# Row halves for the attention scores of a hybrid decoder step: 64 rows of one kv group as both operands, instead of 128 rows with a masked query

## The chip, the cores and the metric

One core of a Trainium2 chip runs the whole program. The metric is the device time of one execution in microseconds (us): the median of 3 runs for the kernel before. The core has five engines that run side by side and meet at semaphores: PE (TensorE, matrix multiply; its weight loads are listed apart, as PEld), DVE (VectorE), ACT (ScalarE), POOL (GpSimd) and SP (SyncE, which here only issues DMAs). Durations of single instructions are given in nanoseconds (ns).

## The reference, cut to what matters

The model computes one step of a decoder trunk for a prompt of 1024 tokens and for 8 samples of 8 tokens. There are 8 query heads in 2 kv groups (4 heads each) of head dimension 64. The change touches the prompt's local attention: for every query token and head, a softmax over the keys of the selected blocks ("sel") and one over a sliding window of 512 ("win"):

```python
def local_attend(q, pos, idx, valid, kv_g, kw, kw_pos):
    ...
    s = jnp.einsum('tghd,tgkd->tghk', q, ks) * SCALE          # sel scores
    o_sel = jnp.einsum('tghk,tgkd->tghd', masked_softmax(s, m_sel).astype(vs.dtype), vs)
    ...
    s = jnp.einsum('tghd,kgd->tghk', q, kw[:, 0]) * SCALE      # win scores
    o_win = jnp.einsum('tghk,kgd->tghd', masked_softmax(s, m_win).astype(kw.dtype), kw[:, 1])
```

A score sums over the 64 dimensions `d` of one kv group `g` only. At 1024 tokens there are 16 blocks of 64 and 16 are selected, so for the prompt the selected branch is plain causal attention over all earlier tokens.

## The kernel before, in words

The program runs in stages: projections, a set-up stage (compressed attention, sums and masks), the prompt's local attention, the samples' attention, then output projection and FFN. Each engine has its own instruction list written out by hand, with semaphores between them. There is no scheduler: the order in the lists is the order of the work.

**Layout.** Queries lie transposed in `qT[:, tile, j, :]`: 128 partitions, of which rows 0 to 63 hold head `j` of kv group 0 and rows 64 to 127 head `j` of group 1, by 128 tokens. Keys lie transposed the same way in `ksT` (selected branch) and `kwT` (window branch): rows 0 to 63 are group 0, rows 64 to 127 group 1.

**Loops.** The prompt attention goes over 8 query tiles of 128 tokens (`QTile`, from i = 7, the tile with the most keys, down to i = 0), and in each over j = 0 to 3. Each (tile, j) has passes. For i of 4 or more there are four: sel group 0, sel group 1, win group 0, win group 1, one unit each. For i below 4 there are two, sel and win, and each holds two units, group 0 and group 1, whose scores go to two neighbouring PSUM banks. That makes 64 passes for i = 7 to 4, and 8 passes for each of i = 3, 2, 1 and 0: 96 in all.

**One step of PE** (`step_of` in `prompt_pe`): turns (`turn`, L778) and applications (`apply`, L790) of the present pass in groups of up to 4 blocks; then the first turn of the next pass; then `scores` (L764) of the pass that is three ahead; then the last `apply` of the present pass. So a group of score matmuls has transposes before it and `apply` matmuls behind it. `scores` issues one matmul for each unit and each 512 columns of keys: 8 blocks of 128 keys make two of 512, a window of 5 blocks makes 512 and 128. All of this is float32, and the profile shows two MATMULs and two LDWEIGHTS for each float32 matmul (a transpose has one).

**The query.** Before the change the sum over 64 dimensions is made with all 128 rows: POOL's `take_q` (L848) makes two copies of the query tile, `q_cur[0]` and `q_cur[1]`, each multiplied by a column `own_rows[:, g]` that is 1 in the rows of its own group and 0 in the others, and `scores` multiplies `q_cur[g]` with all 128 rows of the keys. `own_rows` is filled by four memsets of DVE at the end of the set-up stage (L603). POOL makes the tile of the next j when `s_done` says that the last scores of this j are done, and PE waits for `q_ready` before the first scores of a j.

**Behind the scores.** DVE adds the causal mask and takes the maximum (`highest`, L911 to L916), ACT takes the exponential (`soften`, L873), PE turns the probabilities, DVE and ACT copy them out of PSUM in turns (`save_group`, L829 on DVE and L862 on ACT), PE applies the values, DVE mixes (L928 to L938).

Of the kernel before, what the change touches and what calls it, by code (L numbers as in the profile page):

```python
# [21 lines left out]
ALU = mybir.AluOpType  # L22
# [3 lines left out]
P = 128  # L26
# [12 lines left out]
H, G, HPG, HD = 8, 2, 4, 64  # L39
# [111 lines left out]
def program(nc, a, out):  # L151
    ctx = ExitStack()
    with ctx:
        sem_names = {}

        def sem(name):
            if name not in sem_names:
                sem_names[name] = ctx.enter_context(nc.semaphore(name))
            return sem_names[name]
# [116 lines left out]
        rp = Region(work_at)  # L276
        probs = [rp(SEQ) for _ in range(2)]
        p_cmp_p = arena[:, work_at:work_at + NT * H * NC_P].rearrange("p (t g n) -> p t g n", t=NT, g=G)
        pT = [rp(4, P) for _ in range(2)]
        q_cur = [rp(P) for _ in range(G)]  # L280
        own_rows = rp(G)
        neg_m = rp(4)
        row_sum = rp(4)
        coef = rp(4)
# [27 lines left out]
        def const(name):  # L312
            o, w = CONST[name]
            return cst[:, o:o + w] if o < NEARLY else late[:, o - NEARLY:o - NEARLY + w]
# [31 lines left out]
        def bank(b):  # L346
            return psum[:, b, :]
# [141 lines left out]
        def setup_dve(dve, step, rotate):  # L489
# [4 lines left out]
            for c in range(2):  # L494
                ins = nc.vector.tensor_tensor(
                    prod_p[:, :, c * KV:(c + 1) * KV].rearrange("p t (g d) -> p t g d", g=G),
                    z_all[:, 0:NT, c * KV:(c + 1) * KV].rearrange("p t (g d) -> p t g d", g=G),
                    pos_rep[:, c, :].unsqueeze(1).unsqueeze(1).broadcast_to([P, NT, G, HD]), ALU.mult)
# [7 lines left out]
            for g in range(G):  # L506
                r = slice(g * HD, (g + 1) * HD)
                for b in range(SB):
                    ins = nc.vector.tensor_copy(q_bd[r, b, g * 32:(g + 1) * 32].rearrange("p (j t) -> p j t", j=HPG),
                                                qT[r, NT, :, b * ST:(b + 1) * ST])  # L510
# [17 lines left out]
            for g in range(G):  # L528
                r = slice(g * HD, (g + 1) * HD)
                ins = nc.vector.tensor_copy(ckT_p[r, g, :], bank(6)[r, 0:NC_P])  # L530
# [22 lines left out]
            for i in range(NT):  # L553
                for g in range(G):
                    ins = nc.vector.tensor_tensor(pc[:, i, g * HPG:(g + 1) * HPG],
                                                  bank(4 + i // 2)[:, i % 2 * 256:(i % 2 + 1) * 256].rearrange("p (h g n) -> p g h n", g=G, n=NC_P)[:, g],
                                                  const("cmp_mask")[:, i * NC_P:(i + 1) * NC_P].unsqueeze(1).broadcast_to([P, HPG, NC_P]), ALU.add)
# [6 lines left out]
            for g in range(G):  # L564
                for j in range(HPG):
                    ins = nc.vector.tensor_copy(cv_bd[j * NC_P:(j + 1) * NC_P, g, j * HD:(j + 1) * HD], cv_p[0:NC_P, g * HD:(g + 1) * HD])
# [9 lines left out]
            for b in range(SB):  # L576
                ins = nc.vector.max(m8[0:NS, b, :], cand[0][0:NS, b, :])
            step(ins)
            for b in range(SB):
                ins = nc.vector.match_replace(cand[1][0:NS, b, :], m8[0:NS, b, :], cand[0][0:NS, b, :], -1.0)  # L580
            step(ins)
            step(nc.vector.memset(cand[1][0:NS, :, NCAND:NCAND + 3], 1e30))
            for b in range(SB):
                ins = nc.vector.max(m8[0:NS, SB + b, :], cand[1][0:NS, b, :])
            step(ins)
            for b in range(SB):
                ins = nc.vector.match_replace(cand[2][0:NS, b, :], m8[0:NS, SB + b, :], cand[1][0:NS, b, :], -1.0)
# [10 lines left out]
            step(nc.vector.reciprocal(cmp_sum, cmp_sum))  # L598
            step(nc.vector.tensor_tensor(cmp_sum.rearrange("p (t h) -> p t h", t=NT), cmp_sum.rearrange("p (t h) -> p t h", t=NT),
                                         z_all[:, 0:NT, ZKV - NGATE:ZKV].rearrange("p t (h r) -> p t h r", r=3)[:, :, :, 0], ALU.mult))  # L600
            for g in range(G):
                for h in range(G):
                    nc.vector.memset(own_rows[h * HD:(h + 1) * HD, g:g + 1], 1.0 if g == h else 0.0)  # L603
            nc.vector.memset(coef, 0.0).then_inc(setup_dve_done, 1)

            for i in range(NT):
                dve.wait_ge(pc_applied, i + 1)
                for g in range(G):
                    c = i * H + g * HPG
                    ins = nc.vector.tensor_tensor(mixT[:, 0:HPG, i * P + g * HD:i * P + (g + 1) * HD],  # L610
                                                  bank(i)[:, g * 256:(g + 1) * 256].rearrange("p (j d) -> p j d", j=HPG),
                                                  cmp_sum[:, c:c + HPG].unsqueeze(2).broadcast_to([P, HPG, HD]), ALU.mult)
# [45 lines left out]
        def pooling_act(act):  # L658
# [6 lines left out]
        s_done, m_ready, p_ready, t_done, pv_done, o_used, q_ready = (sem(n) for n in (  # L665
            "s_done", "m_ready", "p_ready", "t_done", "pv_done", "o_used", "q_ready"))
# [82 lines left out]
        def prompt_pe(pe):  # L749
            pe.wait_ge(setup_dve_done, 11)  # L750

            def scores(qt, j, p):
                x = p % 2
                if p == 0:

                    pe.wait_ge(q_ready, j + (4 * qt.pos + 1))

                pe.wait_ge(p_ready, qt.count(j, p) + 1)
                for u, (kind, g) in enumerate(qt.passes[p]):
                    kT = ksT if kind == "sel" else kwT  # L760
                    k0, n = qt.keys[kind]
                    for c in range(0, n * P, 512):
                        w = min(512, n * P - c)
                        ins = pe.matmul(bank(2 * x + u + c // 512)[:, 0:w], q_cur[g],  # L764
                                        kT[:, k0 * P + c:k0 * P + c + w], start=True, stop=True)
                ins.then_inc(s_done, 1)

            def turn(qt, j, p, n):

                x = p % 2  # L770
                y, half, _ = qt.group(j, p, n)
                if n == 0:

                    pe.wait_ge(p_ready, qt.count(j, p) + 3)

                pe.wait_ge(pT_saved[y], half + 1)
                for m, block in enumerate(qt.groups[p][n]):
                    ins = pe.transpose(bank(4 + y)[:, m * P:(m + 1) * P], probs[x][:, block[4]:block[4] + P], ident)  # L778
                ins.then_inc(t_done, 1)

            def apply(qt, j, p, n):
                x = p % 2
                y, half, _ = qt.group(j, p, n)
                pe.wait_ge(pT_saved[y], half + 2)
                if n == 0:

                    pe.wait_ge(o_used, qt.count(j, p) + 1)
                for m, (u, kind, g, kt, _) in enumerate(qt.groups[p][n]):
                    c0 = (KVR if kind == "sel" else 2 * KVR) + KV + g * HD
                    ins = pe.matmul(bank(6 + x)[:, u * HD:(u + 1) * HD], pT[y][:, m, :], z_all[:, kt, c0:c0 + HD],  # L790
                                    start=(kt == qt.keys[kind][0]), stop=(kt == qt.i))
                if n == len(qt.groups[p]) - 1:
                    ins.then_inc(pv_done, 1)

            def step_of(qt, j, p):

                for n in range(1, len(qt.groups[p])):
                    turn(qt, j, p, n)
                    apply(qt, j, p, n - 1)
                nxt, ahead = later(qt, j, p, 1), later(qt, j, p, 3)  # L800
                if nxt:
                    turn(*nxt, 0)
                if ahead:
                    scores(*ahead)
                apply(qt, j, p, len(qt.groups[p]) - 1)

            scores(q_tiles[0], 0, 0)
            scores(q_tiles[0], 0, 1)
            turn(q_tiles[0], 0, 0, 0)
            scores(q_tiles[0], 0, 2)  # L810
            every_pass(pe, step_of)

            pe.wait_ge(o_used, NPASS + 2)
            pe.wait_ge(pT_saved[0], n_groups // 2 + 1)
            pe.wait_ge(pT_saved[1], n_groups // 2 + 1)
            for i in range(NT):
                y = i % 2
                if i >= 2:
                    pe.wait_ge(heads_saved[y], i // 2)
                for k in range(HPG):  # L820
                    ins = pe.transpose(bank(4 + y)[:, k * P:(k + 1) * P], mixT[:, k, i * P:(i + 1) * P], ident)
                ins.then_inc(heads_turned[y], 1)
# [17 lines left out]
        def prompt_pool(pool, behind_first):  # L840

            pool.wait_ge(setup_dve_done, 11)
            qT_flat = qT.rearrange("p t j n -> p (t j) n")

            def take_q(n):

                for g in range(G):
                    ins = nc.gpsimd.tensor_tensor(q_cur[g], qT_flat[:, n, :] if isinstance(n, int) else  # L848
                                                  qT_flat[:, bass.ds(n, 1), :].rearrange("p a n -> p (a n)"),
                                                  own_rows[:, g:g + 1].broadcast_to([P, P]), ALU.mult)  # L850
                ins.then_inc(q_ready, 1)

            take_q(0)
            behind_first()
            for qt in q_tiles:
                with pool.Fori(0, HPG) as j:

                    pool.wait_ge(s_done, qt.count(j, qt.np - 1) + 1)
                    take_q(j + (HPG * qt.pos + 1))
# [1298 lines left out]
```

## Time and profile before

| What | Value |
|---|---|
| median of 3 runs | 1720.71 us (1719.9 to 1721.72) |
| the profiled execution, its own time | 1720.44 us |
| its span, first to last instruction | 1718.6 us |
| mean granted TensorE clock | 0.948 |
| PE busy | 1557.8 us, 91% of the span |
| prompt attention on the time line | about 351 to 641 us |

The span is what the trace covers; the execution's own time is 1.8 us longer. Each row of the profile is for one engine: start, duration, line of the kernel, operation, output and inputs with shapes. "128\*64 128x512" on a matmul means 128 active rows and 64 active columns of the array (the weights), and a moving operand of 128 rows by 512 columns. A matmul's listed duration contains its run through the array and overlaps the next; what it costs in a stream is the distance from its start to the next start. The row of the clock (PEclk) is in tenths of full speed.

### The profile page before, as it was taken

The numbers are of one execution on the slowest core, as the hardware profiler recorded it, in microseconds if no ns is written. First come the engines' busy times: TensorE is split into PE (matmuls) and PEld (weight loads), VectorE is DVE, ScalarE is ACT, GpSimd is POOL, SyncE is SP. The second block draws the span as 40 slices with busy tenths as digits, with TensorE's granted clock in tenths as the row PEclk, the third lists the DMA queues.
The fourth block names the chain that finished last, engine by engine and source line by source line (L and its number), as shares of the span: only waits on it lengthen the run. The fifth ranks groups of instructions, "written<-read, shape, count | busy, mean of one in ns | idle before, by whom it ended". The sixth has DMA issues, their size and how long they took to land.

```text
span 1718.6 us, 26090 instructions
## 1 busy us (share of the span) xinstructions
PE 1557.8 (91%) x9892; PEld 1018.6 (59%) x9892; DVE 781.8 (45%) x1532; ACT 519.9 (30%) x936; POOL 258.3 (15%) x287
## 2 busy tenths in 40 slices
PE   6588985599999988999898999999999999999993
PEld 3244443478887885666354666666666665666662
DVE  5799965567777783665655111111111120100105
ACT  5133220034444544554333122222222221111105
POOL 2244317100000010010320111111111110000002
PEclk9799996599999999999898999999999999999996
DMA  8666632020000005566211111111111111121102
GB/s 365 211 217 210 198 95 84 0 98 1 1 1 1 1 1 220 221 252 190 86 49 35 46 49 49 49 49 49 49 49 49 49 53 48 48 54 34 34 0 116
DMA packets 93460, 146.37 MB, mean 85 GB/s; under 512 B 3691, under 2 KB 74831, under 8 KB 91143
## 3 DMA queue, kind: packets, MB, share of 16 engines
q1 hardware_dynamic: 81823, 78.43, 14.6%
q0 software_dynamic: 11520, 67.11, 11.1%
q8 instruction: 38, 0.62, 0.1%
q14 instruction: 23, 0.19, 0.0%
q10 hardware_dynamic: 56, 0.01, 0.0%
HBM read 135.91 MB, written 14.04 MB: 87 GB/s over the span
## 4 chain that ended last, share of the span: by engine, by line
PE 77%; DVE 15%; DMA 3%; issue 2%; ACT 1%; POOL 1%; SPq 0%; DVEq 0%; POOLq 0%; ACTq 0%
PE psum L1501 43%; PE psum L764 6%; PE psum L790 6%; PE psum L1468 6%; DVE arena L2000 4%; DVE arena L1999 4%; PE psum L778 3%; PE psum L1106 2%; PE psum L1047 2%; PE psum L1059 2%; DMA arena<-in_cache_kv_cmp,cmp_idx 2%; PE psum L1085 1%; PE psum L2070 1%; DMA arena<-in_w_in 1%; PE psum L448 1%
## 5 line engine op out<-in xcount | busy, mean ns | idle before, releaser
L1501 PE MATMUL psum<-arena 128*128 128x384 f16 (+1 forms) x4752 | 734.7, 318 | 5.4 <-POOL arena L1446 2.8
L1501 PEld LDWEIGHTS psum<-arena 128*128 128x128 f16 x4752 | 466.3, 98 | 273.6 <-issue 10.4
L1738 DVE SCALAR_TENSOR_TENSOR arena<-psum,arena 128x384 f32<-128x384 f32 (+1 forms) x66 | 35.3, 535 | 349.2 <-ACT arena L1607 349.2
L2070 PE MATMUL psum<-arena 128*128 128x512 f16 (+1 forms) x768 | 153.6, 361 | 0.0
L790 PEld LDWEIGHTS psum<-arena 128*128 128x128 f32 x1056 | 137.1, 194 | 11.8 <-issue 6.7
L790 PE MATMUL psum<-arena 128*128 128x64 f32 x1056 | 138.7, 268 | 0.0
L1607 ACT ACTIVATE arena<-psum 128x384 f32<-128x384 f32 (+1 forms) x66 | 31.3, 474 | 338.1 <-PE psum L1501 338.1
L764 PE MATMUL psum<-arena 128*128 128x512 f32 (+3 forms) x384 | 130.1, 462 | 1.7 <-DVE arena L610 1.7
L1446 POOL TENSOR_TENSOR arena<-arena 128x384 f32 (+1 forms) x66 | 57.7, 874 | 465.3 <-ACT arena L1609 465.3
L2070 PEld LDWEIGHTS psum<-arena 128*128 128x128 f16 x768 | 76.3, 99 | 73.1 <-issue 5.3
L873 ACT ACTIVATE arena<-psum,arena 128x640 f32<-128x640 f32 (+7 forms) x128 | 89.2, 700 | 56.8 <-DVE arena L916 55.3
L1707 DVE SCALAR_TENSOR_TENSOR arena<-arena 128x2816 f16<-128x2816 f32 x8 | 24.7, 3092 | 173.7 <-ACT arena L1583 173.7
L1468 PE MATMUL psum<-arena 128*128 128x512 f16 (+1 forms) x432 | 97.4, 387 | 4.9 <-POOL arena L1436 4.9
L1850 POOL DMA_INDIRECT arena<-in_cache_kv_cmp,cmp_idx x64 | 78.5, 1226 | 147.7 <-DVE arena L2000 105.2
L778 PE MATMUL psum<-arena 128*128 128x128 f32 x528 | 88.8, 277 | 5.7 <-ACT arena L873 5.7
L764 PEld LDWEIGHTS psum<-arena 128*128 128x128 f32 x384 | 64.5, 191 | 39.8 <-issue 35.1
L916 DVE TENSOR_REDUCE arena<-psum 128x1 f32<-128x640 f32 (+7 forms) x96 | 85.5, 891 | 3.3
L862 ACT ACTIVATE arena<-psum 128x256 f32<-128x256 f32 (+2 forms) x92 | 43.2, 469 | 124.2 <-PE psum L778 117.6
L1632 ACT ACTIVATE arena<-psum 128x384 f32 (+3 forms) x24 | 11.4, 473 | 217.1 <-PE psum L1501 217.1
L1468 PEld LDWEIGHTS psum<-arena 128*128 128x128 f16 (+1 forms) x432 | 43.4, 101 | 55.9 <-POOL arena L1436 5.1
L1172 ACT ACTIVATE arena<-psum 128x512 f32<-128x512 f32 (+2 forms) x104 | 53.1, 557 | 73.8 <-PE psum L1047 47.5
L1703 DVE SCALAR_TENSOR_TENSOR arena<-arena 128x2048 f16<-128x2048 f32 x22 | 50.4, 2292 | 52.3 <-ACT arena L1579 52.3
(259 smaller groups left out, 1643.8 us busy)
## 6 DMA issues: line engine op xcount, KB each, us to landing
arena<-in_w_gate SPq DMA_DIRECT2D x22, 512.0 KB, 4.0
arena<-in_w_up SPq DMA_DIRECT2D x22, 512.0 KB, 5.2
arena<-in_w_down SPq DMA_DIRECT2D x8, 1408.0 KB, 7.1
arena<-in_x_prompt SPq DMA_DIRECT2D x16, 512.0 KB, 3.6
arena<-in_w_in SPq DMA_DIRECT2D x8, 908.0 KB, 12.1
arena<-in_cache_kv_win SPq DMA_DIRECT2D x8, 512.0 KB, 3.3
out_y_prompt<-arena SPq DMA_DIRECT2D x8, 512.0 KB, 2.6
out_kv_win_sample<-in_cache_kv_win SPq DMA_DIRECT2D x1, 4032.0 KB
```

What stands on the lines that cost most here:

```text
L764: ins = pe.matmul(bank(2 * x + u + c // 512)[:, 0:w], q_cur[g], kT[:, k0 * P + c:k0 * P + c + w], start=True, stop=True)
L778: ins = pe.transpose(bank(4 + y)[:, m * P:(m + 1) * P], probs[x][:, block[4]:block[4] + P], ident)
L790: ins = pe.matmul(bank(6 + x)[:, u * HD:(u + 1) * HD], pT[y][:, m, :], z_all[:, kt, c0:c0 + HD], start=(kt == qt.keys[kind][0]), stop=(kt ...
L873: ins = nc.scalar.activation(probs[x][:, u * 512:u * 512 + n], S, ACT.Exp, bias=neg_m[:, 2 * x + u:2 * x + u + 1], accum_out=row_sum[:, 2 ...
L916: nc.vector.tensor_reduce(neg_m[:, 2 * x:2 * x + nu], S[:, :, 0:n * P], AX, ALU.max, negate=True).then_inc(m_ready, 1)
L1446: nc.gpsimd.tensor_tensor(row(1), silu_out[c][:, 0:c1 - c0], row(0), ALU.subtract).then_inc(act_ready, 1)
L1468: ins = pe.matmul(bank(2 * s + h)[0:n, :], mix_slot[s][xp][:, k, 0:n], w_out[wp][:, k, 512 * h:512 * (h + 1)], start=(k == 0 and i == 0), ...
L1501: ins = pe.matmul(out[:, 0:c1 - c0], w[wp][:, k, :], x[xp][:, k, c0:c1], start=(k == 0 and i == 0), stop=(k == n_k - 1 and i == 2))
L1850: nc.gpsimd.indirect_dma_start(raw[k % RAW].rearrange("p c r -> p (c r)"), None, cmp_rows, bass.IndirectOffsetOnAxis(ap=cmp_idx[:, k:k + 1 ...
L1999: step(nc.vector.tensor_tensor(rows, rows, pos, ALU.mult))
L2000: nc.vector.tensor_tensor(cmp_acc, cmp_acc, raw[k % RAW], ALU.add).then_inc(prod_free, 1)
L2070: ins = pe.matmul(dst[:, 0:n], hT[s][xp][:, k, :], w_in[wp][:, k, c0:c0 + n], start=(k == 0 and i == 0), stop=(k == KD - 1 and i == 2))
```

## The change

The 64-row slice `r` of group g is taken from both operands: the query tile and the keys. The zeros are no longer needed, so POOL makes one plain copy of the query tile in place of two masked ones, and the four memsets of `own_rows` go. What is computed is the same. A matmul whose operands start at partition 0 or 64 and have 64 rows addresses the upper or the lower half of the array's rows.

```diff
-        q_cur = [rp(P) for _ in range(G)]
-        own_rows = rp(G)
+        q_cur = rp(P)
...
-            for g in range(G):
-                for h in range(G):
-                    nc.vector.memset(own_rows[h * HD:(h + 1) * HD, g:g + 1], 1.0 if g == h else 0.0)
             nc.vector.memset(coef, 0.0).then_inc(setup_dve_done, 1)
...
                 for u, (kind, g) in enumerate(qt.passes[p]):
                     kT = ksT if kind == "sel" else kwT
                     k0, n = qt.keys[kind]
+                    r = slice(g * HD, (g + 1) * HD)
                     for c in range(0, n * P, 512):
                         w = min(512, n * P - c)
-                        ins = pe.matmul(bank(2 * x + u + c // 512)[:, 0:w], q_cur[g],
-                                        kT[:, k0 * P + c:k0 * P + c + w], start=True, stop=True)
+                        ins = pe.matmul(bank(2 * x + u + c // 512)[:, 0:w], q_cur[r],
+                                        kT[r, k0 * P + c:k0 * P + c + w], start=True, stop=True)
...
             def take_q(n):
 
-                for g in range(G):
-                    ins = nc.gpsimd.tensor_tensor(q_cur[g], qT_flat[:, n, :] if isinstance(n, int) else
-                                                  qT_flat[:, bass.ds(n, 1), :].rearrange("p a n -> p (a n)"),
-                                                  own_rows[:, g:g + 1].broadcast_to([P, P]), ALU.mult)
-                ins.then_inc(q_ready, 1)
+                nc.gpsimd.tensor_copy(q_cur, qT_flat[:, n, :] if isinstance(n, int) else
+                                      qT_flat[:, bass.ds(n, 1), :].rearrange("p a n -> p (a n)")).then_inc(q_ready, 1)
```

## Rows read from the trace of the kernel before

**Rows 1.** The page: PE's busy time and the granted clock in 40 slices.
```profile
PE 1557.8 (91%) x9892; PEld 1018.6 (59%) x9892; DVE 781.8 (45%) x1532; ACT 519.9 (30%) x936; POOL 258.3 (15%) x287
PEclk9799996599999999999898999999999999999996
```

**Rows 2.** Stretch, its us, busy of PE, PEld, DVE, ACT, POOL; PEclk, DMA, GB/s.
```profile
353.00:542.00 189.00, 187.77 (x1305) 152.14 (x1304) 143.75 (x398) 86.51 (x185) 11.45 (x31) 1.00 0.05 22
542.00:602.00 60.00, 60.00 (x399) 47.63 (x397) 44.25 (x114) 29.65 (x80) 6.08 (x16) 1.00 0.00 1
602.00:622.00 20.00, 19.80 (x151) 18.66 (x150) 17.27 (x51) 9.91 (x34) 3.23 (x9) 1.00 0.00 0
622.00:641.00 19.00, 14.82 (x107) 13.13 (x105) 16.44 (x62) 9.91 (x45) 3.61 (x10) 0.91 0.01 2
676.00:816.00 140.00, 136.33 (x1181) 88.88 (x1179) 82.24 (x219) 73.83 (x147) 10.54 (x24) 0.98 0.62 224
```

**Rows 3.** Waits from 542 to 641 us: waiter, releaser, us, times, longest.
```profile
PE psum L778 <- ACT arena L873: 4.0, 9, 0.8
```

**Rows 4.** Time line of PE, i = 7 and then i = 3: start, us, instruction.
```profile
367.89 0.55 PE L790 MATMUL psum<-arena 128*128 128x64 f32 x4
368.28 0.39 PE L778 MATMUL psum<-arena 128*128 128x128 f32 x2
...
559.14 0.61 PE L778 MATMUL psum<-arena 128*128 128x128 f32 x4
559.59 1.88 PE L764 MATMUL psum<-arena 128*128 128x512 f32 x4
561.31 1.00 PE L790 MATMUL psum<-arena 128*128 128x64 f32 x8
562.14 0.61 PE L778 MATMUL psum<-arena 128*128 128x128 f32 x4
```

**Rows 5.** Time line at 298 us: 64-row matmuls, and weight loads in a stream.
```profile
298.07 3.67 PE L440 MATMUL psum<-arena 64*64 64x512 f32 x4 [8.87 <-DVE arena L547]
```

**Rows 6.** Time line of PE in the samples' stage, 690.70 to 690.95 us.
```profile
690.53 0.27 PE L1088 MATMUL psum<-arena 128*128 128x128 f32 x1
690.73 0.27 PE L1089 MATMUL psum<-arena 64*128 64x64 f32 x1
```

**Rows 7.** Time line of PE, samples' stage: 64-row matmuls between 128-row ones.
```profile
693.15 0.43 PE L1117 MATMUL psum<-arena 64*64 64x129 f32 x2
693.51 0.43 PE L1118 MATMUL psum<-arena 128*64 128x128 f32 x2
693.87 1.09 PE L1047 MATMUL psum<-arena 128*128 128x128 f32 x8
```

**Rows 8.** Time line of PE, samples' stage: column halves, and what follows them.
```profile
696.29 1.08 PE L1059 MATMUL psum<-arena 128*64 128x512 f32 x4
697.30 0.66 PE L1085 MATMUL psum<-arena 128*128 128x128 f32 x4
697.79 1.04 PE L1047 MATMUL psum<-arena 128*128 128x128 f32 x8
```

**Rows 9.** Time line of PE, samples' stage: from column halves to a 64-column matmul.
```profile
700.35 1.10 PE L1106 MATMUL psum<-arena 128*64 128x129 f32 x16
701.38 0.43 PE L1073 MATMUL psum<-arena 128*128 128x64 f32 x2
701.66 1.04 PE L1047 MATMUL psum<-arena 128*128 128x128 f32 x8
```

**Rows 10.** Time line at the end of the set-up stage.
```profile
339.17 0.35 DVE L603 MEMSET arena<- 64x1 f32 x4
...
339.68 9.29 PE L463 MATMUL psum<-arena 128*128 128x256 f32 x32 [10.25 <-DVE arena L604]
```

**Rows 11.** POOL's copies of the query tile, and the next scores (i = 0).
```profile
634.12 0.76 POOL L848 TENSOR_TENSOR arena<-arena 128x128 f32<-128x128 f32 x2 [3.00 <-PE psum L764]
...
635.37 0.62 PE L764 MATMUL psum<-arena 128*128 128x128 f32 x4
```

## The prediction

> **What bounds the kernel now.** I read the page first: PE is busy for 91% of the span, and the granted clock is full, outside the set-up stage [rows 1]. Then the table of stretches over the attention stage, because the change lives there: from 353 to 602 us PE is busy for all but 1.2 of 249 us at clock 1.00, DVE for about 75% of it and ACT for less than half [rows 2]. So up to 602 us (tiles i = 7 to 2) whatever PE is given or spared moves the end one for one. From 602 to 622 (i = 1) PE still has 19.8 of 20, but DVE 17.3. From 622 (i = 0) PE is busy 14.8 of 19 and waits 4.0 us, nine times, for ACT's exponential [rows 2, 3]: there a ring of scores, maximum, exponential and turn sets the pace. Last I read the time line of PE, by distances from start to start, in the stage and in the samples' stage, where this kernel already uses 64-row and 64-column matmuls.
>
> **What a score pass costs now.** A 512-column pass of i = 3 is four MATMULs (two matmuls, two passes through the array each) and takes 561.31 - 559.59 = 1.72 us, 0.43 each; the four transposes before it take 0.45 (0.11 each), and the scores begin right behind them [rows 4]. The eight `apply` MATMULs behind take 0.83, and four of them 368.28 - 367.89 = 0.39, so the pace is 0.11 and the first step only 0.05 to 0.06: the first weight loads were made under the scores. A row count of 64 does not shorten a matmul by itself: four of 64x64 by 512 last 3.67 us at the half clock (1.2 GHz) of that stretch, and 4 x 0.43 doubled is 3.42; the 0.25 left is the first load and the run through the array [rows 1, 4, 5]. So what the change can give or take lies in the seams between the forms, and in whether two halves run at once.
>
> **Term 1, the seam into the scores.** Today turn, scores and apply all use the array as 128 by 128. Afterwards scores use 64 rows and their neighbours 128. The trace has this very step: a 128-column transpose with 128 rows, then one with 64 rows, 0.20 us apart, where 0.11 is the distance without a change of form [rows 4, 6]: 0.09 lost. Then the first weight load is no longer under the matmul before: two 64-row MATMULs of 129 columns, with one change of form, take 693.51 - 693.15 = 0.36, and the next pair 0.36 again, where two without a change take 0.22 [rows 7]: 0.14 in all. For the 128-column weights of the scores I take 0.15: 0.093 and a load of 0.056 (L1085: four from 697.30 to 697.79 are 0.49, not 0.436) [rows 8].
>
> **Term 2, the seam out.** Behind the last score comes `apply` with 128 rows. The wait for the array is again 0.095: four 512-column MATMULs of L1059 and the step to L1085 take 1.01, of which two times 0.427 is streaming, 0.055 the exposed load and 0.10 this seam [rows 8]. `apply` moves only 64 columns, so its loads hide worse: after a change of form two such MATMULs take 701.66 - 701.38 = 0.28 [rows 9]; in today's stream the first two take 0.39 - 2 x 0.11 = 0.17 [rows 4]. That is 0.11 more (0.105 unrounded), and the seam out is 0.20.
>
> Together 0.35 us a pass. The three score groups ahead of the loop include two in a row, so there are 95 pairs of seams: 63 in i = 7 to 4, 8 in each of the others. For i = 7 to 4 each pass has one unit; its two matmuls lie in the same half and one behind the other, so nothing is won: 63 x 0.348 = **+21.9 us**. The least that one could argue for is the wait for the array alone, 0.19 a pass; the most, by the 0.36 steps of [rows 7] and one more exposed load for `apply`, 0.40. I take 0.35, whose parts each have a row.
>
> **Term 3, two halves at once.** For i below 4 a pass has both units, group 0 in the upper rows and bank 2x, group 1 in the lower rows and bank 2x+1. No row shows two row halves at once. The nearest show two column halves: four 512-column MATMULs in 1.01 with seam and load, where 1.71 would be the streaming alone, and sixteen of 129 columns in 701.38 - 700.35 = 1.03, 0.064 each instead of 0.11 [rows 8, 9]. Both pairs run at once, though in L1059 both MATMULs of the first half stand ahead of those of the second in the list. The bounds for rows: nothing, or half of the scores' time. I take half, nearest to these rows. i = 3: 8 x (0.348 - 0.854) = **-4.05**. i = 2 (384 columns, 4 x 0.32 = 1.28): 8 x (0.348 - 0.642) = **-2.35**; DVE is at 74 to 75% there [rows 2], so it can follow: a pass of i = 3 falls from 4.28 to about 3.8 with about 3.1 of DVE. i = 1 (256 columns): 8 x (0.348 - 0.43) = -0.65, of which I count **-0.3**, since DVE had only 2.7 of 20 us left. i = 0: PE would pay 0.35 - 0.21, but it waits 4.0 us there anyway; on the ring the scores start 0.15 later and end 0.21 sooner: **0**.
>
> The Trainium skill, TensorEngine Tiling (Array Packing), Key Properties, states that changing the tiling mode, not just the tile, drains the array: the rule that speaks against this change; the steps of 0.20 in [rows 6] agree, and it gives no price. By the same page's theoretical factor of 2 for a dimension of 64 alone one would write off the scores' time to half and forget terms 1 and 2. TensorE: Matmul & The Clock Gate, Part 3, says that a weight load overlaps a running matmul only where the row group differs; by that each one-unit pass would lose three more loads of 0.055, about 10 us in all and 1746. The trace disagrees: in [rows 5] all four have the same rows, and 0.25 beside the streaming has no room for three more loads (0.11 each at that clock).
>
> **Term 4, the rest.** The four memsets of DVE stand ahead of the semaphore for which PE waits 10 us (L463), directly on the path: 0.35 with gaps, 339.17 to 339.56, **-0.4** [rows 10]. POOL's two masked copies (0.76) become one plain copy. No row has a POOL copy of this shape; it lies between nothing and the 0.76 of two, I take about half. It costs nothing either way: POOL starts at 634.12 and the scores that need it at 635.37, in the shortest passes of all, so 1.25 us cover it [rows 11]; if the copy took longer than that, each j of i = 0 would wait for the excess.
>
> **Sum.** +21.9 - 4.05 - 2.35 - 0.3 - 0.4 = +14.8 us. On the profiled execution: 1720.44 (span 1718.6 and 1.84 around it) + 14.8 = 1735.2; that execution is 0.3 under the median, so **1735.5 us** against 1720.71. The likeliest case's own range: a seam pair of 0.32 to 0.40 gives 1733 to 1740.
>
> **Rivals.**
> A. *Row halves don't run at once.* For it: only column halves are seen at once, and row halves share the 128 output columns. Against: they write different banks, and the order in the list did not matter in L1059. Term 3 turns into a loss: 16 x 0.35 for i = 3 and 2 = 5.6, i = 1 up to 2.8, i = 0 about 0.15 a pass on the ring, 1.2: +21.9 + 9.6 - 0.4 = +31, **1752 us** at most, 1749 if i = 1 and 0 hide half. The Trainium skill, TensorE: Matmul & The Clock Gate, Part 3, has four row tiles of 32 at 3.07 times, which speaks against A; no row here shows it.
> B. *The seams are cheap, and it gets faster.* The place is the transpose before and the `apply` behind each score group; the price is 0.35 a pass by the rows, and if halving the rows alone (columns stay 128) let neighbours flow through, it would be near zero. Then -6.8 (i = 3) - 5.1 (i = 2) - 1.5 (i = 1 and 0, DVE and ring) - 0.4 = -14, **1707 us**. It decides at 14 us over some 80 passes that PE bounds: below 0.17 us a pass the kernel is faster. For it: only one of the rows has 128 columns on both sides. Against: exactly that one shows 0.20 [rows 6]. With 0.19 a pass (the wait for the array, loads hidden) it comes out at 1722.
> C. *The array isn't addressed in halves at all*, the instruction just runs with 64 rows live: no seam, no pairs, 0.4 from the memsets, **1720.3 us**. Against it: the 64-row forms of L1117 and L1089 do have seams.
> D. *The clock falls*, half the array being idle in two passes of three. The samples' stage, full of column halves, kept 0.98 [rows 2], and the scores are about a third of the time. If it fell to 1.2 GHz for a fifth of the stage, some 30 us more, 1765.
>
> **How the numbers follow.** Forecast 0.70, A 0.14, B 0.07 (0.03 of it the cheap but not free seam at 1722), C 0.04, D 0.03, rest 0.02 on the slow side. The range should reach A: 1729 to 1752, which leaves out B, C and D, and the ends of the forecast's neighbours. The measurement tells 0.2%, 3.4 us, from no change. Slower: 0.70 + 0.14 + 0.03 + 0.02 = 0.89. Same: C and half of the cheap seam, 0.05. Faster: the rest, 0.06.
>
> **What would show it.** In the changed trace: L764 with 64 active rows; from the last L778 to the first L764 0.20 instead of 0.11, and the second score MATMUL 0.055 later than its streaming time; from the last L764 0.095 beyond its streaming, and the first two L790 0.16 apart. Passes of i = 7 to 4 longer by 0.35 each, in i = 3 four score MATMULs in about 0.91 + 0.1 instead of 1.72. PE's stage starts 0.4 earlier and ends about 14.8 later. It is wrong if the first L764 of a group stands 0.11 behind the transpose (B or C), if in i = 3 the MATMULs are 0.43 apart one by one (A), or if PEclk leaves 1.00 between 353 and 602 (D).

## The result, and the profile after

The changed kernel takes 1929.07 us (median of 4, 1927.8 to 1933.4) against 1720.31: 1.1216 times as long, 95% interval 1.1197 to 1.1236, or 208.8 us more, where 14.8 were forecast. The profiled execution took 1928.32 us with a span of 1926.5. In several kernels below single executions fall into two groups 190 us apart; a ratio with an interval is then over the faster group, and the text gives the single times.

The page of the changed kernel; the rows answer to [rows 1], and the last three are groups of instructions (busy us, mean ns | idle before).

```profile
PE 1768.1 (92%) x9892; PEld 1142.0 (59%) x9892; DVE 784.0 (41%) x1528; ACT 513.1 (27%) x936; POOL 243.0 (13%) x254
PEclk9899975655555555989998989999999999999996
...
L787 PE MATMUL psum<-arena 128*128 128x64 f32 x1056 | 225.1, 375 | 0.0
L761 PE MATMUL psum<-arena 64*128 64x512 f32 (+3 forms) x384 | 203.2, 735 | 1.2 <-DVE arena L606 1.2
...
L775 PE MATMUL psum<-arena 128*128 128x128 f32 x528 | 132.2, 380 | 4.6 <-ACT arena L867 4.5
```

The clock row shows where the time went. In slices 9 to 16 of 40 it reads 5 where it read 9 before; the rest of the row is much as it was. It isn't the scores (L761) alone that grew: `apply` (L787), untouched by the change, has a mean of 375 ns where it had 268, and the turns (L775) 380 for 277. The stretches of the stage, which answer to [rows 2]:

```profile
353.00:763.00 410.00, 409.41 (x1344) 289.77 (x1344) 150.86 (x413) 83.40 (x195) 4.73 (x16) 0.50 0.02 9
763.00:795.00 32.00, 32.00 (x239) 24.58 (x239) 24.89 (x59) 16.60 (x44) 1.48 (x5) 1.00 0.01 1
795.00:822.00 27.00, 27.00 (x208) 20.90 (x207) 23.06 (x67) 14.88 (x47) 1.49 (x5) 1.00 0.00 1
822.00:848.00 26.00, 24.52 (x162) 18.65 (x161) 22.69 (x79) 13.13 (x55) 1.78 (x6) 0.87 0.00 1
```

For 410 us, nearly all of tiles i = 7 to 4, PE is fully busy at a granted clock of 0.50 (1.2 GHz). Once i = 3 has begun, with two units a pass in both halves of the array, it is back at 1.00. Now the start of the stage, PE's time line, first of the kernel before:

```profile
350.69 3.67 PE L764 MATMUL psum<-arena 128*128 128x512 f32 x8 [1.73 <-DVE arena L610]
355.60 0.66 PE L778 MATMUL psum<-arena 128*128 128x128 f32 x4 [1.23 <-ACT arena L873]
```

and of the changed kernel:

```profile
348.69 1.99 PE L761 MATMUL psum<-arena 64*128 64x512 f32 x8 [1.25 <-DVE arena L606]
353.59 1.12 PE L775 MATMUL psum<-arena 128*128 128x128 f32 x4 [2.91 <-ACT arena L867]
354.63 2.50 PE L761 MATMUL psum<-arena 64*128 64x512 f32 x4
```

The first two score groups of the stage, group 0 and group 1 of i = 7, stand side by side in the list. In halves they run at once and are done in 1.99 us instead of 3.67; then PE waits 2.91 us for the first exponential, where it waited 1.23. The clock has fallen by the end of this wait: the four transposes last 1.12 instead of 0.66, and the next four score MATMULs 2.50 instead of 1.25.

Where the clock is high, the forecast's terms can be read. A pass of i = 3 in the changed kernel, beside [rows 4]:

```profile
764.61 0.61 PE L775 MATMUL psum<-arena 128*128 128x128 f32 x4
765.15 1.13 PE L761 MATMUL psum<-arena 64*128 64x512 f32 x4
766.21 0.66 PE L787 MATMUL psum<-arena 128*128 128x64 f32 x4
766.71 0.61 PE L775 MATMUL psum<-arena 128*128 128x128 f32 x4
```

The scores take 1.06 us from start to start where they took 1.72: row halves do run at once. The turns before them take 0.54 instead of 0.45, the seam. The four memsets are gone, and POOL's copy takes 0.30 (mean 296 ns) in place of 0.76.

### The profile page after: what moved, and what is told of

Read it like the earlier page. It is cut to its first block, busy times and chain, and to the rows that moved or that the text cites. A ratio compares the mean times of both kernels' runs of the same rounds, so it can differ in the third digit from the quotient of the medians.

```text
span 1926.5 us, 26053 instructions
## 1 busy us (share of the span) xinstructions
PE 1768.1 (92%) x9892; PEld 1142.0 (59%) x9892; DVE 784.0 (41%) x1528; ACT 513.1 (27%) x936; POOL 243.0 (13%) x254
## 4 chain that ended last, share of the span: by engine, by line
PE 80%; DVE 14%; DMA 3%; issue 2%; ACT 1%; POOL 0%; SPq 0%; DVEq 0%; POOLq 0%; ACTq 0%
PE psum L1495 38%; PE psum L787 10%; PE psum L761 10%; PE psum L775 5%; PE psum L1462 5%; DVE arena L1994 3%; DVE arena L1993 3%; PE psum L1100 2%; PE psum L1041 2%; PE psum L1053 1%; DMA arena<-in_cache_kv_cmp,cmp_idx 1%; PE psum L1079 1%; PE psum L2064 1%; DMA arena<-in_w_in 1%; PE psum L447 1%
## 5 line engine op out<-in xcount | busy, mean ns | idle before, releaser
L787 PEld LDWEIGHTS psum<-arena 128*128 128x128 f32 x1056 | 209.9, 289 | 47.0 <-issue 46.3
L787 PE MATMUL psum<-arena 128*128 128x64 f32 x1056 | 225.1, 375 | 0.0
L761 PE MATMUL psum<-arena 64*128 64x512 f32 (+3 forms) x384 | 203.2, 735 | 1.2 <-DVE arena L606 1.2
L761 PEld LDWEIGHTS psum<-arena 64*128 64x128 f32 x384 | 83.8, 280 | 93.0 <-issue 89.1
L775 PE MATMUL psum<-arena 128*128 128x128 f32 x528 | 132.2, 380 | 4.6 <-ACT arena L867 4.5
L826 DVE COPY arena<-psum 128x384 f32<-128x384 f32 (+2 forms) x88 | 52.3, 594 | 134.2 <-PE psum L775 134.0
L775 PEld LDWEIGHTS psum<-arena 128*128 128x128 f32 x528 | 99.5, 232 | 6.6 <-ACT arena L867 5.2
L905 DVE TENSOR_TENSOR psum<-psum,arena 128x128 f32<-128x128 f32 (+1 forms) x96 | 33.0, 344 | 120.2 <-PE psum L761 117.2
L844 POOL COPY arena<-arena 128x128 f32 (+1 forms) x33 | 9.8, 296 | 529.1 <-PE psum L761 486.7
```

What stands on the lines that cost most here:

```text
L761: ins = pe.matmul(bank(2 * x + u + c // 512)[:, 0:w], q_cur[r], kT[r, k0 * P + c:k0 * P + c + w], start=True, stop=True)
```

## The experiments

Three theories. **R**: half-row passes that leave half of the array's rows idle cannot hold the clock. **S**: the changes of form, by their drains, or 64-row matmuls as such, lower it. **H**: half-row passes hold whichever level they find; what lets it fall is the start of the stage.

To compare stages I take from each trace the distance from the first maximum (DVE's reduction behind the scores) of a tile to that of the next, for the profiled execution, in us; the last column is to the last maximum of the stage:

```
kernel                    i=7    i=6    i=5    i=4    i=3    i=2    i=1    i=0
before                   53.1   51.1   46.6   43.4   31.5   26.6   20.2   14.2
changed                 108.5  108.5   99.5   91.6   30.1   24.9   20.0   13.7
pairs only               53.1   51.1   46.6   42.8   28.1   24.9   20.0   14.1
singles only            107.0  108.5   99.6   92.9   31.5   26.6   20.2   14.3
column halves            58.1   56.7   52.1   48.9   34.3   29.3   21.0   14.0
i = 7 in full rows       53.3   57.4   52.8   48.8   28.1   24.9   20.0   14.1
primed, 12               66.1   57.4   52.8   48.8   28.1   24.9   20.0   13.7
first groups in full     58.4   57.4   52.8   48.8   28.1   24.9   20.0   14.3
serial start             76.6   57.4   52.8   48.8   28.1   24.9   20.0   13.7
swapped halves           49.5   48.7   44.4   42.3   28.1   24.9   20.0   13.6
```

**1. Pairs only.** Row halves where they come in pairs, from the kernel before:

```diff
+                        r = slice(g * HD, (g + 1) * HD) if qt.np == 2 else slice(0, P)
-                        ins = pe.matmul(bank(...)[:, 0:w], q_cur[g], kT[:, ...], start=True, stop=True)
+                        ins = pe.matmul(bank(...)[:, 0:w], q_cur[g][r], kT[r, ...], start=True, stop=True)
```

> The kernel before (two masked query tiles), with row halves only in the 32 passes of i = 3 to 0, whose two units fill both halves of the array; the 64 one-unit passes of i = 7 to 4 stay at 128 rows. Theory R (the clock falls because half of the array's rows stand idle in the one-unit passes): the clock stays at 1.00 to the end of the stage, L764 of i = 3 goes from 4.28 to about 3.8 us a pass and i = 2 from 3.2 to about 2.95, together some 6 us: 1714, and not above 1716. Theory S (the changes of form themselves, by their drains, lower the clock): the clock falls in i = 3 to 0 too and the time is over 1760. Theory H (the clock had fallen for another reason near 353 us and only could not rise again): says nothing against 1714.

Measured: 1715.09 us against 1720.92, ratio 0.9968 (0.9957 to 0.9979). The stretch over i = 7 to 4 and most of i = 3, in the columns of [rows 2]:

```profile
355.00:590.00 235.00, 235.00 (x1662) 188.83 (x1661) 180.86 (x497) 110.79 (x254) 17.43 (x46) 1.00 0.03 11
```

The clock stays at 1.00 in spite of the 32 changes of form; R and H as expected, S not. This part of the change is a gain of 5.8 us.

**2. Singles only.** The same line with `qt.np == 4`.

> The opposite half: row halves only in the 64 one-unit passes of i = 7 to 4, full 128 rows in i = 3 to 0, masked query tiles kept. Theory R: the clock falls near 353 us and stays at 0.50 up to i = 3, as in the changed kernel; the time is that of the changed kernel plus the 6 to 7 us that the pairs saved there: 1929 + 7 = 1936. If the pairs had a part in the fall of the clock, the time would be clearly under 1929.

Measured: 1933.3, 1934.1, 1935.8 and one execution of 1746.3 us.

```profile
351.00:355.00 4.00, 1.23 (x6) 0.82 (x7) 3.35 (x5) 2.29 (x4) 0.23 (x1) 1.00 0.85 356
355.00:359.00 4.00, 4.00 (x20) 3.44 (x18) 1.71 (x6) 1.50 (x5) 0.00 (x0) 0.56 1.01 434
359.00:755.00 396.00, 396.00 (x1299) 281.00 (x1298) 144.41 (x397) 78.46 (x183) 12.13 (x32) 0.50 0.01 2
```

The loss is all in the one-unit passes, as R expected. But R has no place for the fourth execution. The same program, with the same half-row passes, took a time that only a full clock allows; its mean granted clock was 0.946, against 0.845 to 0.849 in the other three. That, and the fall right behind the stretch in which PE is busy 1.23 of 4 us, speaks for H.

**3. Column halves.** Each score matmul of the kernel before in two halves of 64 query tokens, with all 128 rows:

```diff
+                        for h in range(2):
+                            ins = pe.matmul(bank(...)[h * 64:(h + 1) * 64, 0:w], q_cur[g][:, h * 64:(h + 1) * 64],
+                                            kT[:, k0 * P + c:k0 * P + c + w], start=True, stop=True)
```

> The kernel before with each score matmul split in two column halves (64 query tokens each, output to partitions 0 to 63 and 64 to 127), all 128 rows, masked query: as many changes of form as in the changed kernel, the whole array occupied, and no gain from pairs. Theory R: clock 1.00; 95 seam pairs of 0.35 to 0.40 us, less the slack of i = 0: +30 to +38, 1751 to 1759. Theory S: the clock falls as in the changed kernel, and the time is over 1900.

Measured: 1748.57 us, ratio 1.0167 (1.0151 to 1.0183), a little under the expected band.

```profile
355.00:660.00 305.00, 304.53 (x2278) 210.43 (x2278) 212.95 (x594) 128.72 (x325) 22.75 (x60) 1.00 0.03 11
```

As many changes of form as in the changed kernel, in all of i = 7 to 0, and the clock stays at 1.00: the drains don't lower it, and 64-row matmuls as such didn't in experiment 1. S falls. The table gives the seams as 5.5 us per 16 passes (i = 6, 5 and 4), 0.34 each, with weights of 64 columns.

**4. i = 7 in full rows**, halves from i = 6 on (`qt.i != 7` in the line of experiment 1).

> The kernel before with row halves in all passes but the 16 of i = 7, which keep 128 rows (masked query tiles kept). So the stage starts with some 50 us of full-row work, and the half-row passes of i = 6 to 4 begin at full clock. Theory H (half-row passes can hold a clock that is high, but cannot bring back one that has fallen; the fall is owed to the start of the stage, where PE waits 3.5 us for the first maximum): the clock stays at 1.00 all through, 47 seam pairs of 0.40 and 6 less from the pairs: 1734. Theory R (half-row passes cannot hold it): the clock falls soon after i = 6 begins and stays at 0.50 to the start of i = 3, some 145 us more: 1870 to 1885.

Measured: 1732.11 us (1731.3 to 1735.2), ratio 1.0067 (1.0054 to 1.0080), 2 us under the forecast.

```profile
405.00:565.00 160.00, 160.00 (x996) 117.57 (x995) 110.25 (x313) 63.83 (x144) 9.10 (x24) 1.00 0.00 1
```

This is i = 6 to 4 with nothing but half-row scores, 48 passes over 160 us, at 1.00. R falls: such passes do hold the clock, if they find it high.

**5. Primed.** The changed kernel with extra work in the wait at the start, never read:

```diff
             scores(q_tiles[0], 0, 1)
+            for k in range(12):
+                pe.matmul(bank(4 + k % 2), q_cur, kwT[:, 0:512], start=True, stop=True)
             turn(q_tiles[0], 0, 0, 0)
```

> The changed kernel with 12 matmuls of 128 rows by 512 columns, float32, put between the second score group and the first turn, their results never read: they fill PE's 3.5 us of waiting at the start of the stage, and cost the rest, 12 x 0.854 less 3.5 = 7 us, at full clock. Theory H: the clock stays at 1.00 after them, 1735 + 7 = 1742. Theory R: it falls one or two readings later, 1929 + 7 = 1936.

> The primed kernel with 4 extra matmuls (3.4 us of work, about the length of the wait) in place of 12. Theory H: the clock holds and the extra work hides in the wait: 1738 to 1740. If it takes more full-row work than that to carry the clock into the half-row passes: 1929, or some runs at either.

Measured: 1745.44 us with 12 (ratio 1.0138, 1.0123 to 1.0153), 3 us over the forecast, and 1739.93 with 4 (1.0107, 1.0092 to 1.0122), as forecast; no execution was above 1746. With 12:

```profile
351.00:363.00 12.00, 12.00 (x33) 5.13 (x30) 2.96 (x4) 2.41 (x4) 1.67 (x2) 1.00 0.87 350
363.00:590.00 227.00, 227.00 (x1417) 165.85 (x1415) 155.73 (x430) 92.06 (x206) 5.33 (x18) 1.00 0.00 1
```

With 4 the clock is at 1.00 from 347 to 580 us as well. Four matmuls of no use make the changed kernel 189 us faster.

**6. The first three score groups**, which stand ahead of the loop, by themselves: in full rows while all others are halves, and the reverse. From the kernel before:

```diff
+                        r = slice(g * HD, (g + 1) * HD) if not (qt.pos == 0 and isinstance(j, int) and j == 0) else slice(0, P)
```

(and the same without `not`.)

> The kernel before with row halves everywhere but in the first three score groups of the stage (i = 7, j = 0, ahead of the loop). In the changed kernel the first two of them lie in different halves and run at once, so PE is done after 1.8 us in place of 3.5 and then waits 3.1 us for ACT where it waited 1.5 before. Theory H (it is this start that lets the clock fall, and half-row passes hold a high clock but cannot raise a low one): the clock holds, 1739 (the single execution of the singles-only kernel at full clock, 1746, less 6 to 7 for the pairs). Theory R (half-row passes cannot hold it from the start on, and what helped in the primed and in the i = 7 kernels was their 10 to 50 us of full-row work): 1929.

> The kernel before with row halves in nothing but these first three score groups. [...] If a low clock needed more than full-row work to come back, the time would be over 1850.

Measured: 1738.97 us (1736.6 to 1740.0), ratio 1.0104 (1.0088 to 1.0119), and 1722.18, ratio 1.0011 (1.0002 to 1.0020). First the kernel with these groups in full rows, then the one with only these in halves:

```profile
351.00:355.00 4.00, 2.99 (x7) 0.96 (x6) 2.46 (x4) 1.03 (x2) 1.37 (x2) 1.00 0.75 258
355.00:580.00 225.00, 224.78 (x1403) 164.59 (x1403) 154.92 (x427) 91.37 (x205) 13.64 (x36) 1.00 0.04 15
```

```profile
351.00:355.00 4.00, 1.09 (x7) 0.27 (x4) 2.96 (x4) 1.23 (x3) 0.98 (x2) 1.00 0.84 283
355.00:359.00 4.00, 4.00 (x20) 3.23 (x20) 2.24 (x6) 2.38 (x4) 0.00 (x0) 0.72 1.02 434
359.00:363.00 4.00, 4.00 (x28) 3.52 (x27) 2.43 (x7) 0.53 (x3) 0.76 (x2) 0.85 0.78 332
363.00:600.00 237.00, 237.00 (x1632) 191.56 (x1632) 178.14 (x489) 110.06 (x253) 16.67 (x44) 1.00 0.00 1
```

The pair of kernels separates the two parts of H. Three score groups of 96 in full rows keep the clock in all four executions and are worth 190 us. These three alone in halves bring it down too in the profiled execution, some 2 us behind the end of the same wait of 2.91 us, but with 128-row passes behind them it is back at 1.00 before 363 us, and the median is only 1.8 us higher.

**7. The changed kernel again**, and **with a serial start**:

```diff
             scores(q_tiles[0], 0, 0)
+            pe.wait_ge(s_done, 1)
             scores(q_tiles[0], 0, 1)
```

> The changed kernel itself once more, to see whether single executions escape the fall, as one of four of the singles-only kernel did (1746 beside 1933). Theory H: the outcome hangs on how the readings of the clock gate lie to the wait at the start of the stage, so a run near 1739 may turn up beside those near 1929. A theory in which half-row passes as such pull the clock down allows only 1929.

> The changed kernel with one wait more: PE begins the second score group of the stage only when the first is done, so the first two groups no longer run at once. The start is all half-row work, but PE is busy with it for 3.6 us and then waits about 1.3 us, as before the change. If the longer wait (2.9 us in place of 1.2) lets the clock fall: it holds, 1740. If it is that the work at the start has half of its rows idle or that too little was done, with whatever wait: 1929, or some executions at either.

Measured: the changed kernel five times at 1925 to 1931 and once at 1780.2 us. The profiled one of these, at 1929.67, repeats the first trace: a wait of 2.91 us, then the clock at 0.50 to the start of i = 3, and 408.1 us for i = 7 to 4. The serial start: 1734.9, 1735.1, 1735.8 and 1736.5; 1755.5; 1928.7 and 1931.5. Its ratio without the last two is 1.0088 (1.0073 to 1.0102). The profiled execution is the one of 1755.5:

```profile
350.20 6.21 PE L761 MATMUL psum<-arena 64*128 64x512 f32 x8 [1.25 <-DVE arena L606]
356.34 1.12 PE L775 MATMUL psum<-arena 128*128 128x128 f32 x4
```

```profile
351.00:355.00 4.00, 3.94 (x6) 1.34 (x5) 1.52 (x2) 0.74 (x1) 1.25 (x2) 0.57 0.76 262
...
367.00:391.00 24.00, 24.00 (x80) 16.66 (x79) 8.09 (x21) 5.11 (x11) 0.00 (x0) 0.50 0.00 1
391.00:411.00 20.00, 20.00 (x122) 14.70 (x122) 12.31 (x33) 6.62 (x15) 0.58 (x2) 0.96 0.00 0
411.00:500.00 89.00, 89.00 (x546) 64.40 (x546) 58.38 (x160) 34.92 (x75) 1.76 (x6) 1.00 0.00 0
```

Neither answer holds alone. Without the long wait four of seven executions keep the clock, where the changed kernel kept it in none of ten; but it can fall even so. Here PE had waited only 1.25 us, and the clock fell within the first two score groups, which stretch to 6.21 us. And this trace corrects H: some 40 us later, still in half-row passes of i = 7, the clock comes back. So half-row passes can bring it back, but seldom do: the changed kernel's two traces have 410 us without it. The execution of 1780 has no trace; its mean granted clock of 0.923 lies between 0.845 and 0.948, and an estimate from its 43 us above 1737 is a low stretch of some 90 us, since the changed kernel loses 190.8 us in 408.1.

**8. Swapped halves.** The idle half put to use. POOL keeps a second copy of the keys (in the then free `summ`) and of the query with the groups' rows exchanged; a one-unit pass gives its first blocks to its own rows and the others to the opposite rows. The first part ends at the end of its bank, so that the scores stay one run of columns. The edit also unrolls POOL's loop over j and moves POOL's first gathers for the samples from the start of the stage to the start of i = 3; what these do alone was not run.

```diff
+                    if qt.np == 4:
+                        o, w0 = slice((1 - g) * HD, (2 - g) * HD), (n + 1) // 2 * P
+                        pe.matmul(bank(2 * x)[:, 512 - w0:512], q_cur[r], kT[r, k0 * P:k0 * P + w0], start=True, stop=True)
+                        ins = pe.matmul(bank(2 * x + 1)[:, 0:n * P - w0], q_sw[o], k_sw[kind][o, k0 * P + w0:(k0 + n) * P], start=True, stop=True)
+                        continue
```

> The changed kernel, with the one-unit passes of i = 7 to 4 spread over both halves of the array: POOL keeps a second copy of keys and query with the groups' rows exchanged, and each pass gives the first half of its key blocks to its own rows and the second half to the other rows, in two neighbouring banks, so that the scores stay in one run of columns. The same number of changes of form as in the changed kernel. Theory R or H (idle rows cost the clock): the clock stays at 1.00 and the two halves run at once: scores of 8, 7, 6, 5 blocks take 0.85, 0.85, 0.64, 0.64 us instead of 1.71, 1.49, 1.28, 1.07, less 0.40 a pass: -3.6, -1.9, -1.9, -1.1, and -6 in i below 4: 1706. Theory S (64-row work as such or its drains cost the clock): half clock as in the changed kernel, over 1850.

The single executions lay between 1703.0 and 1714.6, and in the profiled one the clock is low for a short stretch near 353 us. So the same kernel was run with the four extra matmuls of experiment 5 as well:

> [...] If the start is what scatters it: no low reading at 353, about 2 us less, 1704 to 1705 and no execution above 1709. If the extra work is not hidden: up to 3.4 us more, 1710.

Measured: 1706.67 us, ratio 0.9919 (0.9900 to 0.9938), and with the four extra matmuls 1706.28, ratio 0.9917 (0.9904 to 0.9931), executions from 1703.1 to 1707.8, a little over the 1704 to 1705 expected. The first one's time line, a pass of 8 blocks, and its stretch:

```profile
380.32 0.69 PE L766 MATMUL psum<-arena 64*128 64x512 f32 x1
380.33 0.69 PE L767 MATMUL psum<-arena 64*128 64x512 f32 x1
380.86 0.59 PE L766 MATMUL psum<-arena 64*128 64x512 f32 x1
380.86 0.59 PE L767 MATMUL psum<-arena 64*128 64x512 f32 x1
381.38 0.66 PE L797 MATMUL psum<-arena 128*128 128x64 f32 x4
```

```profile
351.00:355.00 4.00, 2.38 (x6) 1.13 (x8) 0.87 (x4) 0.00 (x0) 0.87 (x3) 0.74 0.00 0
355.00:359.00 4.00, 2.76 (x14) 0.89 (x10) 3.44 (x6) 2.39 (x4) 0.00 (x0) 0.83 0.00 0
359.00:600.00 241.00, 241.00 (x1774) 179.81 (x1773) 194.77 (x533) 118.32 (x281) 18.96 (x60) 1.00 0.05 18
```

The two halves start 0.01 us apart, the scores of 1024 columns take 1.06, and from 359 us the clock is at 1.00. With as many seams as the changed kernel this one is 14 us faster than the kernel before, and with its primed form the fastest of the study; the table gives 9.3 us of it in i = 7 to 4 and about 6 in the rest. The stretches say more: the clock fell here too, at the start (0.74 and 0.83), and was soon back with passes behind it that use both halves. And it fell with the DMA share at 0.00. In the kernels above it lies between 0.31 and 1.05 from 351 to 359 us, whether the clock holds or falls. So transfers are not needed for the fall. With the four extra matmuls:

```profile
347.00:351.00 4.00, 1.98 (x7) 0.97 (x7) 1.13 (x4) 0.00 (x0) 0.87 (x3) 0.81 0.00 0
351.00:355.00 4.00, 4.00 (x11) 1.36 (x8) 3.05 (x4) 1.41 (x3) 0.00 (x0) 0.76 0.00 0
```

The low stretch is still there, only earlier, in place of the "no low reading" expected: it lies in the first score groups, which begin at 349.47 after a wait of 2.02 us, and the extra matmuls begin at 353.07, behind it. So they could not prevent it. The medians differ by less than the runs can tell; that the highest execution went from 1714.6 to 1707.8 may be chance.

## Why the prediction was wrong, by its own steps

**The step that failed is rival D**, "the clock falls, half the array being idle in two passes of three". The outcome was named, with its sign (PEclk leaving 1.00 between 353 and 602), and given 0.03 and 30 us; the mechanism was named only in part, since the same passes with half of the array idle ran at 1.00 for 160 us in experiment 4. What the runs showed in its place: the clock falls at the start of the stage, and one-unit half-row passes rarely bring it back. D was dismissed by the samples' stage, "full of column halves", at 0.98 [rows 2]. But those stand in pairs that fill the array [rows 8, 9], as do i = 3 to 0 and the column halves of experiment 3. The nearest rows of before with part of the array idle and PE busy are short, like the 3.67 us of [rows 5], so the row cited could not bear on it. The price had no row behind "a fifth of the stage" either. At the lower level PE's work takes nearly twice the time (1.89 times in i = 6), and in the changed kernel's two traces the low stretch lasts until the work changes: at full clock i = 7 to 4 take 58.4 + 57.4 + 52.8 + 48.8 = 217.3 us unrounded (first groups in full), in the changed kernel 408.1. The difference, 190.8, is nearly all of the miss of 194.

**Overlooked was the start.** The prediction counted the two adjacent groups ahead of the loop as one seam less, but not that they lie in opposite halves. Term 3 applied to them gives 1.7 us of work taken out of a stretch in which PE then waits, behind a clock that had risen only some 6 us before the stage began (from 339 to 343 us it was still 0.51). Whether this nearness matters was not tried.

**The forecast's own terms**, at full clock (first groups in full, against before): i = 7 to 4 +23.1 of 21.9 forecast. A seam pair costs 6.2 / 16 = 0.39, not 0.348. The mis-sized part is the exposed load, sized from a form with 64-column weights (L1059) and one with 128 rows (L1085). In the kernel with i = 7 in full rows:

```profile
425.28 0.61 PE L779 MATMUL psum<-arena 128*128 128x128 f32 x4
425.82 1.34 PE L765 MATMUL psum<-arena 64*128 64x512 f32 x4
427.10 0.66 PE L791 MATMUL psum<-arena 128*128 128x64 f32 x4
427.59 0.50 PE L779 MATMUL psum<-arena 128*128 128x128 f32 x3
```

Into the scores 0.54 for 0.44, as forecast. The four, two of 512 and two of 128 columns, take 1.28, of which 1.07 is streaming and 0.095 the seam out: 0.11 exposed, not 0.055. `apply` has 0.49 for 0.39 [rows 4], as forecast. The single starts in the trace show where: the second MATMUL of the group stands 0.53 behind the first, the third 0.43 behind the second and the fourth 0.11 behind the third. So only the first step has an exposed load, and inside the group the loads stay hidden. The Trainium skill, TensorE: Matmul & The Clock Gate, Part 3, has in its list of what overlaps that loads are hidden only under another row group; the trace disagrees here too, as these four share their rows. The Trainium skill, TensorEngine Tiling (Array Packing), Key Properties, puts a drain at a change of mode; the trace agrees, with 0.095 on either side. The pairs: i = 3 -3.4 (forecast -4.05), i = 2 -1.7 (-2.35), i = 1 -0.2 (-0.3), i = 0 nothing (0). The sum at full clock is about +18, and three kernels show it: 1739.0, 1739.9, and 1735 to 1737 for the serial start. All are inside the range and within 4.4 us of 1735.5. The seams cost 1.2 us more than forecast and the pairs gave 1.4 us less: two small misses that go the same way.

**Rival A** (halves not at once) fell: 1.06 for 1.72 in i = 3. So did B and C: the seams are there. Term 4: PE's last set-up matmuls started 1.99 us earlier in this profile. The memsets were 0.35 in [rows 10]; the rest is start-up scatter between executions and was not separated. The copy by POOL takes 0.30, and no wait of PE for it shows among those of i = 3 to 0.

**What stays open.** Why the clock falls in some executions of the serial start and not in others, and what brought it back after some 40 us in one, isn't settled: the traces show one execution of each kernel, two of the changed one. Nor was it tried whether a single column half would act like a single row half, or whether unread work in the idle half alone would bring the clock back. And which part of the start lets the clock fall is not settled either. In the four traces with a wait of 2.9 us and nothing in it the clock falls in the wait or within 2 us behind it; in the serial start and in both swapped kernels it fell behind waits of 1.25 and 2.02 us.

## What to carry to other kernels

Use a row half of TensorE only together with the other one: in pairs the same change is a gain (1715 for the pairs alone, 1706 with every pass paired), alone it saves nothing, pays 0.39 us for each change of form and back, and mostly leaves the clock where it finds it. Before a change that thins out PE's work, look at what stands at the start of the stage: where PE works for a few us and then waits, a few matmuls moved or made shorter can decide the clock of all that follows. And a median over executions with one clock can hide a second outcome: read the single times and the clock row before any sum of instructions.

## What the hardware showed that was not expected

- One program with two outcomes 190 us apart, by chance: 1746.3 beside 1933 to 1936; 1735 to 1737 and 1755.5 beside 1929 and 1932.
- The same half-row passes run for 160 us at 2.4 GHz if they begin there, and 410 us at 1.2 GHz if they don't.
- Four extra matmuls, 3.4 us of work, save 189 us.
- The fall at the start also comes where both halves are used (swapped halves, 0.74 in 351 to 355 us); there the clock is back by 359 us.
- Of a 64-row form with 128 columns of float32 weights 0.11 us of loads is exposed behind a change of form; of the 128-row form it was 0.055 [rows 8].
